# Seven projection stages of a tuned transformer kernel start on the un-normed residual stream

## What is computed

```python
def rms_norm(x, gain=None):
    y = xf * lax.rsqrt(jnp.mean(xf * xf, axis=-1, keepdims=True) + EPS)
def modulate(h, shift, scale):
    return h * (1.0 + scale) + shift
def swiglu(h, w_in, w_out):
    gate, up = jnp.split(h @ w_in, 2, axis=-1)
    return (jax.nn.silu(gate) * up) @ w_out
...
x = x + 0.5 * m_lat[:, 2] * swiglu(modulate(rms_norm(x), m_lat[:, 0], m_lat[:, 1]), ffn_in[l, 0], ffn_out[l, 0])
h_lat = modulate(rms_norm(x), m_lat[:, 3], m_lat[:, 4])
```

## Time and profile before

| | us |
|---|---|
| three runs | 2743.47, 2746.32, 2752.06 |
| median | 2746.32 |
| the profiled execution | 2751.04 |
| its span | 2749.3 |
| PE busy | 2506.5 (91%) |
| DVE busy | 1653.3 (60%) |
| ACT busy | 1010.4 (37%) |
| POOL busy | 385.6 (14%) |

### The profile page before, as it was taken

The page is one execution under the profiler, slowest core; times in us unless marked ns, Lnnn a source line. Parts: engine busy times, 40 slices in busy tenths (PEclk is TensorE's granted clock), DMA queues, the critical chain, the costliest instruction groups (busy, mean ns, idle before and its releaser), DMA issues.

```text
span 2749.3 us, 48927 instructions
## 1 busy us (share of the span) xinstructions
PE 2506.5 (91%) x19458; PEld 2056.1 (75%) x19458; DVE 1653.3 (60%) x2697; ACT 1010.4 (37%) x1630; POOL 385.6 (14%) x342
## 2 busy tenths in 40 slices
PE   6999999978888899999899999879999998789976
PEld 4888877747777678888788887669997865567856
DVE  3777776465555477778677743565544335544665
ACT  4222223353332342222422223355444244434344
POOL 2000010114351200000100001011023500020041
PEclk9999999989999999999999999999999999889998
DMA  6666662200000256666466643125652320023401
GB/s 258 225 192 191 199 182 84 74 1 4 4 4 4 79 158 191 195 192 203 143 192 195 192 143 96 58 81 157 180 177 78 99 88 23 1 61 119 127 8 46
DMA packets 88428, 323.47 MB, mean 118 GB/s; under 512 B 9712, under 2 KB 10864, under 8 KB 87504
## 3 DMA queue, kind: packets, MB, share of 16 engines
q1 hardware_dynamic: 86864, 310.68, 36.6%
q0 software_dynamic: 1408, 10.59, 1.1%
HBM read 320.17 MB, written 1.05 MB: 117 GB/s over the span
## 4 chain that ended last, share of the span: by engine, by line
PE 83%; DVE 8%; ACT 5%; issue 2%; DMA 1%; DVEq 1%; POOL 0%; ACTq 0%; SPq 0%
PE bank L392 22%; PE bank L394 22%; PE bank L393 22%; PE bank L1841 3%; PE bank L1126 1%; DMA weight_ring<-stream_k 1%; DVE row_statistics L1167 1%; PE bank L1117 1%; PE bank L2415 1%; PE bank L1140 1%; ACT work L1228 1%; PE bank L1509 1%; ACT work L1237 1%; ACT weights_hi_lo L344 1%; DVE weights_hi_lo L349 1%
## 5 line engine op out<-in xcount | busy, mean ns | idle before, releaser
L344 ACT ACTIVATE weights_hi_lo<-weight_ring 128x1024 fp32r<-128x1024 f32 (+1 forms) x388 | 404.0, 1042 | 1186.3 <-PE bank L394 1175.5
L392 PE MATMUL bank<-input_hi,weights_hi_lo 128*128 128x512 f32 (+1 forms) x2080 | 769.3, 370 | 46.7 <-DVE input_lo L638 41.4
L349 DVE TENSOR_TENSOR weights_hi_lo<-weight_ring,weights_hi_lo 128x1024 fp32r<-128x1024 f32 (+1 forms) x372 | 452.8, 1217 | 570.4 <-ACT weights_hi_lo L344 569.6
L393 PE MATMUL bank<-input_lo,weights_hi_lo 128*128 128x512 f32 (+1 forms) x2080 | 765.5, 368 | 0.0
L394 PE MATMUL bank<-input_hi,weights_hi_lo 128*128 128x512 f32 (+1 forms) x2080 | 765.2, 368 | 0.0
L392 PEld LDWEIGHTS bank<-input_hi,weights_hi_lo 128*128 128x128 f32 x2080 | 400.5, 193 | 119.3 <-issue 52.6
L393 PEld LDWEIGHTS bank<-input_lo,weights_hi_lo 128*128 128x128 f32 x2080 | 400.1, 192 | 63.1 <-issue 0.5
L394 PEld LDWEIGHTS bank<-input_hi,weights_hi_lo 128*128 128x128 f32 x2080 | 399.5, 192 | 63.4
L392 PE MATMUL bank<-hidden_hi_lo,weights_hi_lo 128*128 128x512 f32 (+1 forms) x960 | 345.3, 360 | 27.5 <-DVE hidden_hi_lo L902 17.6
L393 PE MATMUL bank<-hidden_hi_lo,weights_hi_lo 128*128 128x512 f32 (+1 forms) x960 | 343.7, 358 | 0.0
L394 PE MATMUL bank<-hidden_hi_lo,weights_hi_lo 128*128 128x512 f32 (+1 forms) x960 | 343.5, 358 | 0.0
(11 more groups left out here) (475 smaller groups left out, 2861.9 us busy)
## 6 DMA issues: line engine op xcount, KB each, us to landing
weight_ring<-stream_k SPq DMA_DIRECT2D x498, 512.0 KB, 3.6
weight_ring<-stream_f SPq DMA_DIRECT2D x64, 448.0 KB, 3.4
weight_ring<-stream_f SPq DMA_DIRECT2D x32, 512.0 KB, 3.7
extra_tiles<-condrows POOLq DMA_DIRECT2D x3, 1024.0 KB, 5.3
constants<-consts POOLq DMA_DIRECT2D x1, 2112.5 KB, 9.0
residual_stream<-xin SPq DMA_DIRECT2D x1, 2048.0 KB, 12.5
work<-nabias POOLq DMA_DIRECT2D x1, 2048.0 KB, 8.5
residual_stream<-ctx POOLq DMA_DIRECT2D x1, 1024.0 KB, 7.1
```

The source lines that it names most:

```text
L344: act.activation(split_place(place)[:, 0, 0:words], w[:, 0:words], ACT.Copy).then_inc(hi_ready, 1)
L349: eng.tensor_tensor(split_place(place)[:, 1, 0:words], ring[:, n % RING, 0:words], split_place(place)[:, 0, 0:words].bitcast(F32), ALU.sub ...
L392: pe.matmul(out, weights[:, 0, w], x_hi, start=first, stop=False)
L393: pe.matmul(out, weights[:, 0, w], x_lo, start=False, stop=False)
```

## The change

For the norms 1 to 7 the first slab of the stage is no longer multiplied with the normed input.

- In the tail of the stage in front, ACT writes `H_HI` = round(X * scale) for each tile right behind its square (`raw_hi`), and DVE `H_LO` = X * scale - `H_HI` (`raw_lo`). The slab's own split goes to a new place of its own (`FIRST`), so ACT need not wait for PE with it.
- PE, behind the last product of the stage in front, first multiplies the slab in plain float32 with the shift, two columns wide (`shift_product`, 8 matmuls), then the raw tiles 0 and 1 with the slab (`raw_product`), then sums the squares, then takes the raw tiles 2 to 7.
- The norm itself goes on as before and writes `H_HI` and `H_LO` again, each tile once PE has read the raw one. The normed pair of slabs is now the second and the third, in place of the first and the second.
- The root is now written to SBUF (`RMS`, tile 8 of `BIG`, whose name in a trace is projections), since `pb[bank + 1]` takes the shift's product. This holds for all norms, norm 0 and the final one too.
- DVE copies the shift's product (`first_shift`), and behind the norm multiplies the raw result by `RMS` into `RAW_OUT`; ACT adds the shift's product and applies what the stage wants (Silu in an FFN, a copy in a linear stage).
- In the FFNs 1 and 2 POOL loads the condition rows once the raw product is done, and ACT takes their Silu behind the first gate's, in place of ahead of it. The slab's ring slot is released by the raw product, in place of by its split.
- The squares of the norms 1 to 7 go round in four tiles in place of eight.

```diff
+RAW_FIRST = 2
...
+        RMS, RAW_OUT = BIG[:, 8, :], WORK[:, 11, :]
...
+        def raw_product(pe, n, kts):
+
+            a, b = NORMS[n][0]
+            if n in NORM_BEHIND_MIXER:
+                pe.wait_ge(mixer_added, 4 + NORM_BEHIND_MIXER.index(n) * KT + 5)
+            for kt in kts:
+                pe.wait_ge(input_split[0], split_by_vector_before(n) + kt + 1)
+                mm = split_product(pe, pb[0][:, a:b], FIRST, kt, H_HI[:, kt, a:b], H_LO[:, kt, a:b], kt == 0, kt == KT - 1)
+                mm.then_inc(summed if kt < KT - 1 else slab_done, 1)
+
+        def shift_product(pe, n):
...
+            w = take(pe, first_slab(stage, 0))
+            pe.wait_ge(mods_ready, MODS_OF_NORM[n])
+            pe.wait_ge(first_ready, FIRST_AT[stage][0] + 1)
+            for kt in range(KT):
+                pe.matmul(pb[bank + 1][:, 0:2], w[:, kt * P:(kt + 1) * P], MODS[:, shift + kt, :], start=kt == 0, stop=kt == KT - 1)
...
+        def raw_hi(act, n, kt):
...
+            for s, p, q in segments(cols):
+                ins = act.activation(H_HI[:, kt, p:q], X[:, kt, p:q], ACT.Copy, scale=MODS[:, scale + kt, s:s + 1])
+            ins.then_inc(modulated, 1)
+
+        def raw_lo(dve, n, kt):
...
+            dve.drain()
+            dve.wait_ge(modulated, raw_modulated(n, kt))
+            for s, p, q in segments(cols):
+                ins = dve.scalar_tensor_tensor(out=H_LO[:, kt, p:q], in0=X[:, kt, p:q], scalar=MODS[:, scale + kt, s:s + 1],
+                                               in1=H_HI[:, kt, p:q].bitcast(F32), op0=ALU.mult, op1=ALU.subtract)
+            ins.then_inc(input_split[0], 1)
...
-            act.activation(pb[bank + 1][:, a:b], WORK[:, 0, a:b], ACT.Exp, scale=-0.5).then_inc(rooted, 1)
+            act.activation(RMS[:, a:b], WORK[:, 0, a:b], ACT.Exp, scale=-0.5).then_inc(rooted, 1)
...
         def norm_tensor(pe, n):
+            if n:
+                shift_product(pe, n)
+                raw_product(pe, n, range(RAW_FIRST))
+                if n == 6:
+                    two_norms_tensor(pe)
             sum_squares(pe, NORMS[n][0], NORMS[n][3], NORMS[n][4])
+            if n:
+                raw_product(pe, n, range(RAW_FIRST, KT))
...
-                                                       scalar=MODS[:, scale + kt, s:s + 1], in1=pb[bank + 1][:, p:q],
+                                                       scalar=MODS[:, scale + kt, s:s + 1], in1=RMS[:, p:q],
...
+            if n:
+                dve.wait_ge(slab_done, DONE_AT[stage][0] + 1)
+                dve.tensor_tensor(RAW_OUT[:, a:b], pb[0][:, a:b], RMS[:, a:b], ALU.mult).then_inc(scaled, 1)
+                dve.drain()
...
+                    if first and f and k == 0:
+                        act.wait_ge(hidden, 1 + f * FT + 1)
+                        act.wait_ge(scaled, scaled_before(FFN_NORMS[f]) + KT + 1)
+                        for s, c, e in segments((a, b)):
+                            ins = act.activation(GATE[:, c:e], RAW_OUT[:, c:e], ACT.Silu, bias=first_shift[:, s:s + 1])
+                        ins.then_inc(gated, 1)
+                        if mods_beside(f):
+                            condition_scalar(act, f)
...
+            pool.wait_ge(slab_done, DONE_AT["ffn_in2"][0] + 1)
+            pool.dma_start(EXTRA[:, :, :], condrows[:, 1, :]).then_inc(cond_loaded, 16)
             norm_gpsimd(pool, 3)
-            pool.wait_ge(mod_read, MOD_BATCHES[4][1] - FIRST_MODS)
-            pool.dma_start(EXTRA[:, :, :], condrows[:, 1, :]).then_inc(cond_loaded, 16)
```

More of the change, by code:

```diff
@@ L382, in first_products @@
+            if not norm:
+                pe.wait_ge(first_ready, FIRST_AT[stage][0] + 1)
+            pe.wait_ge(split_ready, VECTOR_SPLIT_AT[stage][0] + pair[1])
             for kt in range(KT):
                 wait_input(pe, norm, kt)
-                for m in range(2):
-                    mm = split_product(pe, pb[m][:, a:b], m, kt, H_HI[:, kt, a:b], H_LO[:, kt, a:b], kt == 0, kt == KT - 1)
+                for m in pair:
+                    place = first_place(stage, m)
+                    mm = split_product(pe, pb[m][:, a:b], place, kt, H_HI[:, kt, a:b], H_LO[:, kt, a:b], kt == 0, kt == KT - 1)
@@ L569, in norm_scalar @@
             else:
-                last_squares(act, cols, x_ready, x0, stage)
+                last_squares(act, place, cols, x_ready, x0, stage, n)
             if n != 6:
@@ L590, in norm_scalar @@
                     ins.then_inc(modulated, 1)
-        ADDED_PLACES = list(range(len(NORMS) + len(GAIN_NORMS)))
         def add_squares_gpsimd(pool, cols, place):
@@ L938, in product @@
                 mm.then_inc(slab_done, 1)
-            product(2, 2, None, 0)
+            if norm:
+                pe.wait_ge(gated, f * FT + 3)
+            else:
+                product(2, 2, None, 0)
             product(3, 3, None, 0)
@@ L1021, in turn @@
                         split_lo(dve, k, slabs[k - 2][0], s1 + k - 1, slabs[k - 2][1])
+                    elif first and f and k < 2:
+                        if k == 0:
+                            split_lo(dve, 1, n + each + 2, s0 + 4)
                     elif not first or k:
@@ L1028, in turn @@
                     if mods_beside(f):
+                        if first and k == 0:
+                            dve.wait_ge(cond_ready, f + 1)
                         mod_product(dve, n + 2 * k + 3, k, i, 8)
@@ L2976, in last_read @@
                     by_gpsimd = gpsimd_splits(stage)
+                    if q == 0 and stage in NORM_STAGES:
+                        return slab_done, DONE_AT[stage][0] + 1, 0
                     if q < by_gpsimd:
```

216 lines of the change are left out of this document (148 added, 68 removed).

## The result

| | before | changed |
|---|---|---|
| median of the runs, us | 2744.9 (4 runs) | 2764.15 (4 runs) |
| all runs | 2743.47 to 2752.06 | 2761.44 to 2768.85 |
| the profiled execution | 2751.04 | 2761.44 |
| ratio, 95% interval | | 1.007 [1.0055, 1.0085] |

The changed kernel is 0.7% slower, 19 us by the medians. I had forecast 8.6 us faster, 2738, in a range of 2722 to 2751, and had given slower by over 0.3% a chance of 0.16. The time lies above the range, beyond what rival D gave and inside what rival C gave.

What follows compares the result with a forecast made beforehand. PE, busy 91%, was taken as the bound, with norm waits and half clock behind them. Terms 12.0 + 0.4 + 1.3 - 2.8 - 0.8 - 1.5 gave 8.6 us faster: 2738 from median 2746.32, range 2722 to 2751.

Steps and rivals of the forecast that it cites:

- rival D: Raw product starts 2 to 3 us late at sites 2 and 7, awaiting POOL's low part; 2743, chance 0.17.
- rival C: Short waits at the sites keep PE's clock at half through most of the pair; 2760, slower, chance 0.18.
- the gap, and half clock behind it: PE waits some 6 us for each norm, then runs at half clock, costing some 2; gain bounded at 6.4 a site.
- The port: Norm scalings with two SBUF operands are held by POOL's subtraction: 0.75 a round, pair's end from 19.5 to 21.8.
- Norm 0: First norm, without a raw product, also reads the root from SBUF: two rounds of 0.75 show, 1.5 us slower.
- The chain of the first turns: Sites 2 and 3: gate, condition's Silu, modulation products, hidden tile, fifth split; PE idles 4.4, plus 2.0 for half clock.
- Eight float32 matmuls of two columns take 1.05: PE's shift product, ahead of the raw tiles at each site of norms 1 to 7, costs 1.05 us.
- The ones take 1.14: PE's two matmuls with ones, summing the squares behind raw tiles 0 and 1, take 1.14 us.
- The mark: Third product's end at site 1, counted from the last product in front: 25.7 us before, forecast 21.8.
- end at about T0: Sites 2 and 7: POOL's low part of the first slab ends about when the last product in front does; uncosted.
- What I had costed at nothing: ACT's and DVE's raw parts in the tails, 0.9 us each per tile, covered by over 2 us idle time.
- S: Experiments' theory: the condition's Silu holds FFN 1 and 2's first turns; PE waits 4.1 us at site 2, 4.4 at 3.

Runs made afterwards that it cites:

- e2: Changed kernel with the root also written to its PSUM bank for the scalings, and the shift's product in another bank; 2743.3 us, ratio 0.9998 to the kernel before.
- e7: Changed kernel with the shift's product between raw tiles 6 and 7, and DVE's copy of it behind the norm; 2745.1 us, ratio 0.9996 to the kernel before.
- e3: Changed kernel with the first slab's split one product earlier on ACT and POOL at sites 2, 5, 6 and 7; 2747.3 us, ratio 1.0005 to the kernel before.
- e5: Changed kernel without PE's wait for the first gate ahead of an FFN's fourth product; 2763.5 us, ratio 1.006 to the kernel before.
- e8: Changed kernel with all parts together: e2, e3, e7, e4, e5 and e6; 2722.5 us, ratio 0.9913 to the kernel before.
- e4: Changed kernel with DVE's hidden tile and its split ahead of the modulation products in FFN 1 and 2's first turn; 2763.4 us, ratio 1.0059.
- e6: Changed kernel with FFN 1's first-slab split in free hidden tiles, so the condition is loaded and its Silu taken before site 2; 2764.9 us, ratio 1.0059.
- e9: Changed kernel with three parts together: e2, e3 and e7; 2727.0 us, ratio 0.9932 to the kernel before.
- e0: The changed kernel run again unaltered, as zero point; 2765.9 us, ratio 1.006 to the kernel before.

## Why the prediction was wrong

**What held.** What bounds the kernel (the gap, and half clock behind it) was right: mended, the change takes 5.8 us from sites 1 and 4, where I had put the limit at 6.4. The port was right in kind, place and size: 0.74 from one row pair of the earlier trace rows, rounds of 3.4 us, 2.4 us at sites 1 and 4 in e2 where I had 2.3; here the trace and the Trainium skill (GPSIMD Engine Reference, section 1. Specifications, on DVE instructions with two SBUF inputs) agree. On ACT the root's new place cost 0.02 (exp 0.63 for 0.61), within the less than 0.1 that I had given it. Norm 0 came at +1.3 for +1.5, by luck with the loads: from the first slab's split on it grew by 2.0. The chain of the first turns was right in its steps.

**The step that failed first: "Eight float32 matmuls of two columns take 1.05", and "The ones take 1.14".** The eight take 1.84. I read x8 as eight matmuls, and they were four with two records each. The ones take 1.92, since 1.14 was one matmul of the two. Both stand ahead of the root at every site, and so on the whole chain, and each is some 0.7 us too small: at site 1 the root was ready at T0 + 6.3 (T0 = 410.9) and not 4.9, the first normed tile at 9.2 and not 8.0, and the pair ended at 23.4 in place of 21.8. The mark moved 2.3 us, and not 4. e7 shows that the place matters: moved behind the ones, the shift's product gives 1.5 to 1.8 back at sites 1, 3 and 4. What the ones cost has no experiment of its own; it is read from the rows.

**The second: the waits for POOL's low part of `FIRST`.** I had costed this at 2 to 3 us for site 5 alone, and made it a rival for sites 2 and 7 with a chance of 0.17. It came at all three and at site 6, which I had not looked at: 7.6 us in all. My timeline had it "end at about T0", and in a sum that goes by half microseconds that should have been a cost in the forecast. The work in the tail made it later by 0.9 us at sites 2 and 7 and by 1.3 at site 5, which I had not looked for.

**The third: the clock behind these waits.** I took half clock for the gaps of 3 us and more in the first turns, and none for a wait of 1.2 us followed by tiny products. At sites 2, 6 and 7 six raw matmuls stood 0.46, 0.41 and 0.46 us apart in place of 0.25, and the shift's product took up to 3.54. e3 takes the second and the third away together: 15.2 us over four sites, that is 7.6 of waits, and as much again of what follows them. Of the 24.7 us between forecast and trace 9.5 are left in e3, 1.0 to 2.6 at every site but the fifth, where nothing is; at site 1 it is the 1.7 of the first step.

**Sizes in the first turns.** Site 2 was +6.8 for +2.8, and site 3 +1.3 for -1.3: the chain starts later by the steps above and by a wait of 0.85 us ahead of the fourth product, which the sum leaves out; at site 5 it was 1.80. It is for the fourth slab's split, which ACT begins only behind the norm and the table load (e5).

**What I had costed at nothing** in the tails did not lengthen them: up to the last product in front they are as long as before at every site, and sites 1 and 4 give 5.8 us in e8. But behind a mixer it made POOL's split late, as told above. The probabilities were at fault with the sums: three terms (tiny matmuls and ones, a split that ends at about T0, the clock) all lay on the side of slower, and the range took in only one at a time.

**Open.** e4, e5 and e6 are too small to be told apart one by one; together they are the 4 to 5 us between e9 and e8, whose intervals just overlap. By site the two traces differ by 3.9 us at site 2 and 3.0 at site 3, where e4 and e6 have their edits, so something of S holds. Why the half clock lasts longer in one execution than in another was not settled: at site 6 the same wait of 2.89 us ahead of the fourth slab was followed by a granted clock of 1.00 in the changed kernel's trace and of 0.51 in e0's, and this is some 4 us. What the clock costs in the odd stretches far from the sites (5.8 us in the even mixer between two executions) is not of this change.

## What to carry to other kernels

When work is put into a gap, ask what it needs at the gap's first instant: the wait for the norm went, and PE stood instead for a split that had had 7 us of slack. Whatever stands ahead of the step that starts the long chain is paid in full, however small, so put it where the chain is running already. And a cost on an engine beside the bound (here the port) is worth little while the bound is slow, and its full price once the bound is mended: the same 22.6 us of DVE were 5 us in the kernel before, and 17 to 20 in the changed one.

## What the runs showed of the hardware

- A float32 matmul shows as two records (x16 for the shift's eight, x2 for one with ones); with two columns a record takes 0.115 us at full clock (1.84 us for sixteen), and 0.22 at half (3.54 for sixteen at site 5).
- Waits of 1.15 to 1.80 us followed by the shift's product were followed by a granted clock of 0.50 in six of six traces, at sites 2, 6 and 7; waits of 1.05 to 1.71 us followed by the raw matmuls at once (e7) by 1.00, and the shift's product without a wait (e3) by 1.00. A wait of 3.42 us was followed by 0.50 by itself (e7, site 5); the wait of 2.89 us at site 6 was followed once by 1.00 (changed kernel) and once by 0.51 (e0).
- Over the 120 scalings of 128x256 a scalar_tensor_tensor took 660 ns on average with both operands in SBUF and 475 ns with one in PSUM. Those beside POOL's subtraction take the difference: four of them 2.71 us, against 1.66 with POOL idle.
